# Down projection of an expert's last 32 slots on four quarters of the array's columns

## What is computed

```python
for e in range(N_EXPERTS):                                   # 16
    h = jax.nn.silu(xf @ w_gate[e]) * (xf @ w_up[e])         # 1024 -> 256
    out = out + gate[:, e:e + 1] * (h @ w_down[e])           # 256 -> 1024
x = layer_norm(ALPHA * x + out, ln2_g, ln2_b)
```

## Time and profile before

| | us |
|---|---|
| timed executions | 1508.08, 1513.96, 1527.37 |
| span of the profiled execution | 1520.2 |
| TensorE busy in the span | 1318.4 |
| first to last matmul of the experts | 1114.6 to 1439.3 |
| first gather of `combine` | 1446.2 |

### The profile page before, as it was taken

The page is one execution under the profiler, slowest core; times in us unless marked ns, Lnnn a source line. Parts: engine busy times, 40 slices in busy tenths (PEclk is TensorE's granted clock), DMA queues, the critical chain, the costliest instruction groups (busy, mean ns, idle before and its releaser), DMA issues. The chain is left out here.

```text
span 1520.2 us, 16147 instructions
## 1 busy us (share of the span) xinstructions
PE 1318.4 (87%) x5597; PEld 813.6 (54%) x5597; DVE 775.7 (51%) x1787; ACT 398.4 (26%) x805; POOL 431.7 (28%) x460
## 2 busy tenths in 40 slices
PE   5898899999999999999898997996289999999800
PEld 2566565755656656656654544653156666666500
DVE  0024125778778878988897988333300000000078
ACT  1142424324324224224314212311011111111111
POOL 5103024052151251261055012002231111113487
PEclk9999899999999898999898988575679999999955
DMA  8966645536543443443333333001078766667163
GB/s 272 313 200 210 231 145 179 173 108 201 155 159 123 146 147 112 146 147 108 113 113 122 110 94 118 1 14 29 4 252 301 235 218 234 211 203 250 35 221 121
DMA packets 146265, 238.60 MB, mean 157 GB/s; under 512 B 17211, under 2 KB 117474, under 8 KB 146194
## 3 DMA queue, kind: packets, MB, share of 16 engines
q1 hardware_dynamic: 131298, 197.66, 40.3%
q0 software_dynamic: 10064, 29.16, 5.9%
q10 hardware_dynamic: 4832, 10.88, 2.3%
HBM read 211.38 MB, written 26.29 MB: 156 GB/s over the span
## 5 line engine op out<-in xcount | busy, mean ns | idle before, releaser
L1188 PE MATMUL bank_pair<-win,xT 128*128 128x384 f32 (+7 forms) x1152 | 450.6, 542 | 14.8 <-DMA win<-in_w_in 13.7
L1188 PEld LDWEIGHTS bank_pair<-win,xT 128*128 128x128 f32 (+1 forms) x1152 | 213.3, 193 | 192.0 <-issue 100.9
L897 DVE MAX8 top<-score 128x8 f32<-128x384 f32 (+6 forms) x201 | 174.9, 870 | 4.0
L898 DVE MATCH_REPLACE8 score<-top,score 128x384 f32<-128x384 f32 (+6 forms) x201 | 171.9, 855 | 0.0
L1282 PE MATMUL bank_pair<-w_out,yT 128*128 128x512 f32 (+1 forms) x288 | 131.2, 610 | 0.4 <-ACT yT L623 0.4
L1641 DVE COPY rows<-bank_pair 32x1024 f32<-32x1024 f32 x16 | 19.4, 1212 | 170.3 <-PE bank_pair L1677 170.3
L567 POOL TENSOR_TENSOR small<-small,pexp 128x4 f32<-128x4 f32 (+1 forms) x9 | 9.4, 1049 | 335.9 <-DVE small L1078 335.9
L1677 PE MATMUL bank_pair<-wd,hT 128*128 128x512 f32 (+1 forms) x192 | 98.8, 653 | 0.0
L1551 POOL DMA_INDIRECT xg<-x_rows,ids x32 | 30.1, 941 | 229.1 <-PE bank_pair L1656 215.9
L1282 PEld LDWEIGHTS bank_pair<-w_out,yT 128*128 128x128 f32 (+1 forms) x288 | 52.8, 186 | 74.0 <-issue 72.2
L1142 PE MATMUL bank_pair<-ident,lm 128*128 128x128 f32 (+2 forms) x234 | 43.2, 312 | 45.8 <-ACT lm L733 15.8
(11 more groups left out here) (339 smaller groups left out, 2091.7 us busy)
## 6 DMA issues: line engine op xcount, KB each, us to landing
win<-in_w_in SPq DMA_DIRECT2D x90, 768.0 KB, 4.4
win<-in_w_in SPq DMA_DIRECT2D x18, 1024.0 KB, 5.3
win<-in_w_in SPq DMA_DIRECT2D x18, 840.0 KB, 5.2
win<-in_w_in SPq DMA_DIRECT2D x18, 800.0 KB, 4.6
wg<-in_w_exp_gate SPq DMA_DIRECT2D x12, 1024.0 KB, 6.2
wu<-in_w_exp_up SPq DMA_DIRECT2D x12, 1024.0 KB, 9.4
wd<-in_w_exp_down SPq DMA_DIRECT2D x12, 1024.0 KB, 11.1
expert_rows<-rows ACTq DMA_DIRECT2D x16, 512.0 KB, 3.3
```

Of the source, the lines that this page charges most:

```text
L897: step(V.max(top8[0:n], sc))
L898: step(V.match_replace(sc, top8[0:n], sc, NEG))
L1188: last = mmul(zb[0:n, 0:w], xT[:, kk, 0:n], win[:, i % NWIN, k, 0:w], start=(kk == 0), stop=(kk == KD - 1))
```

## The change

The 32 slots of OB are computed on all four quarters of the array's columns. Quarter `q` (columns 32q to 32q + 31) holds the same 32 columns of `hT` and multiplies the quarter `q` of `wd`'s 1024 columns (`DQ` = 256 of them), so that its output lies on partitions 32q to 32q + 31 of PSUM: 128 partitions of 256 instead of 32 partitions of 1024. There are 8 matmuls with 256 moving columns where there were 4 with 512, that is 16 MATMUL records instead of 8. OA is done with both halves `f` first, then OB with both. VectorE's copy takes 128 x 256, and the store writes each slot's row in four pieces of 1 KB instead of one of 4 KB.

```diff
+QB = 128 // CB
+DQ = D // QB
@@ ScalarE
-                    act.dma_start(rows_e[128:CAP, bass.ds(e, 1), :].rearrange("s one d -> s (one d)"), rows[j % 2][0:CB, 1, :]).then_inc(S(f"rows_stored{j % 2}"), 16)
+                    act.dma_start(rows_e[128:CAP, bass.ds(e, 1), :].rearrange("s one (q d) -> q s (one d)", q=QB),
+                                  rows[j % 2][:, 1, 0:DQ]).then_inc(S(f"rows_stored{j % 2}"), 16)
@@ VectorE
-                        V.tensor_copy(rows[j % 2][0:CB, 1, :], OB[0:CB, :]).then_inc(S("ob_copied"), 1)
+                        V.tensor_copy(rows[j % 2][:, 1, 0:DQ], OB[:, 0:DQ]).then_inc(S("ob_copied"), 1)
@@ TensorE
+                    pe.wait_ge(S("oa_copied"), e + 1)
                     for f in range(2):
                         pe.wait_ge(S("h_ready"), e * 2 + (f + 3))
-                        for out, c0, nb, sem in ((OA, 0, 128, "oa"), (OB, 128, CB, "ob")):
-                            if f == 0:
-                                pe.wait_ge(S(sem + "_copied"), e + 1)
-                            for c in range(2):
-                                last = E.matmul(out[0:nb, 512 * c:512 * c + 512], hT[:, f, c0:c0 + nb], wd[j][:, f, 512 * c:512 * c + 512],
-                                                start=(f == 0), stop=(f == 1))
-                            if f == 1:
-                                last.then_inc(S(sem + "_ps"), 1)
+                        for c in range(2):
+                            last = E.matmul(OA[:, 512 * c:512 * c + 512], hT[:, f, 0:128], wd[j][:, f, 512 * c:512 * c + 512],
+                                            start=(f == 0), stop=(f == 1))
+                    last.then_inc(S("oa_ps"), 1)
+
+                    pe.wait_ge(S("ob_copied"), e + 1)
+                    for f in range(2):
+                        for q in range(QB):
+                            last = E.matmul(OB[CB * q:CB * q + CB, 0:DQ], hT[:, f, 128:CAP], wd[j][:, f, DQ * q:DQ * q + DQ],
+                                            start=(f == 0), stop=(f == 1))
+                    last.then_inc(S("ob_ps"), 1)
```

## The result

The change takes 1465.89 us in the median of four executions (1457.91 to 1472.87), where the kernel before took 1513.89 beside it; the ratio is 0.9662, with a 95% interval from 0.9621 to 0.9704. A second measurement, beside one of the experiments, gave 0.967 [0.9618, 0.9723]. The profiled execution has a span of 1470.9 us where before had 1520.2, that is 49.3 less.

The account below looks back on a forecast made before the run. TensorE's work bounds the experts' stretch: 16 x (2.56 + 0.31) = 45.9, plus 0.8, plus 6.6, makes 53.3 us off 1513.96, so 1461 us. Likeliest case 1453 to 1474; up to 1485, about 8 in 10.

Parts of the forecast that it names:

- part 1: OB's streaming in the down projection: four quarters run at once, 0.88 us instead of 3.44, saving 2.56 us a body.
- part 2: Order in the down projection: OA, then OB, leaves two changes of shape instead of four, saving 0.31 us a body.
- two halves in L1397: Sign for part 1: L1397's heads alternate between array halves and overlap fully, a pair each 0.08 us; assumed for four quarters.
- The two rules of the Trainium skill: Against OB's overlap: weight loads overlap matmuls only across row groups (sum about nothing); matmuls start and end in program order (1480).
- strict order: Within rival two at a time: OB's records start strictly in order, 8 or 9 rounds, about 1480 us; rival's chance 0.17.
- part 5: Clock falls behind the experts' transposes: three instead of seven, 6.6 us saved; bounds 11.5 saved to 13.1 lost; softest term.
- part 3: OB's copy and store: copy 0.40 us instead of 1.21, saving 0.8 us once before `combine`; store's effect taken as 0.
- part 4: Shorter body of 16.84 us squeezes weight loads, gathers and GpSimd's scaling; all stay covered, cost 0, GpSimd's cover some 4 us.

Follow-up runs that it names:

- the run with the order alone: Against the kernel before: OA with both f, then OB with both f, OB still on one quarter; ratio 1.0054 [1.0017, 1.0092].
- the quarters outside: Against the change: OB's loops turned round, both f for each quarter before the next quarter; ratio 0.9732 [0.9678, 0.9786].
- four stores: Against the change: OB's store issued as four stores, one for each quarter, instead of one with outer dimension four; 1474.0 us in one execution.

## Why the prediction was right

The forecast was 53.3 us less (1461 us); the medians differ by 48.0 (1465.89 us), the profiled executions by 49.3, and the ratio makes 51.

- The streaming (part 1): right to 0.01 us. Together with the order (part 2) a body was to shrink by 2.87 us to 16.84; it did. The order's share is the 0.31 us of the run with the order alone, the quarters' share the rest. What the prediction drew from two halves in L1397 holds for four quarters. The two rules of the Trainium skill that it weighed (TensorE: Matmul & The Clock Gate, Part 3, "What overlaps and what doesn't") don't hold here: four records with four weight loads on the same rows start together, and four rounds are measured where strict order would need nine, or thirteen with the quarters outside.
- The clock (part 5): three falls taken, three measured, and that is luck. From the start of the first to the start of the last matmul of the experts it is 324.2 us before (1114.6 to 1438.9; the table's 1439.3 is neither that start nor the end, 1439.5) and 272.1 after (1116.2 to 1388.3), 52.1 less, for 45.9 + 6.6 = 52.5. But the three was chosen between none and 15 without a working, and the argument for fewer falls, that a body of another length doesn't keep step with them, isn't borne out: the run with the order alone, a body shorter by 0.31 us, got three falls more, and bodies of 16.84 us with seven or ten would have cost 6.6 or 11.5 us more. That the falls need the transposes in one piece is shown by cutting them; how many falls a length of body meets is not explained by the runs (19.71 us: seven; 19.39 and 19.41: ten; 17.68: six; 16.86 and 16.84: three).
- The end (part 3): the term that was mis-sized. It was to save 0.8 us and cost 1.9 (9.14 us from the last matmul's start to the gather for 7.27). The copy is right (0.42 us for 0.40); the store was set at nothing, within 1 us, and cost 1.9 + 0.8 = 2.7. The step that failed is that it looked at the size of the pieces and not at the shape of the store, whose outer dimension of four keeps it to four DMA engines.
- What the shorter body squeezes (part 4): nothing became late. GpSimd's scaling ends at 1385.04, 3.7 us before VectorE's last copy starts, for some 4 expected, and the DMA engines' share of 0.76 over the stretch (0.65 before) left TensorE waiting no more than before:

```profile
1360.36 24.68 POOL L1564 TENSOR_SCALAR xr<-xr 128x1024 f32<-128x1024 f32 x9 [19.31 <-DMA b<-in_ln_b]
```

The time that a gather has was worked out wrongly, though harmlessly: it is asked for when the transposes of expert `e - 1` are done and needed for those of `e + 1`, two bodies less the transposes themselves, 30 us, not 11.

- The rest of the difference is 1.6 us by which the trunk, which isn't touched, ended later in the profiled execution of the change, less 0.6 us in `combine`: 52.1 - 1.9 - 1.6 + 0.6 = 49.2. The trunk moves by much more between executions. The first matmul of the experts starts at these times in the run with the order alone and in that with four stores:

```profile
L1668 PE MATMUL bank_pair<-xgT,win x256: 299/299/630, 1101.1 to 1357.3; 128*128 128x160 f32 x128
```

```profile
L1670 PE MATMUL bank_pair<-xgT,win x256: 299/299/629, 1118.7 to 1334.1; 128*128 128x160 f32 x128
```

That is 17.6 us apart for the same trunk, nearly as much as the 19 us between the kernel before's own executions. Up to these starts TensorE has 4078 matmul records in both, busy for 982.95 us at a mean granted clock of 0.89 in the first and for 998.52 us at 0.88 in the second: most of the difference is TensorE's time, and the granted clock is the lower one there; why it differs isn't shown. A term of 5 us is read from the stretch and not from the total.

## What to carry to other kernels

Where TensorE is the bound and an output fills only a quarter of the array's columns, spread its moving columns over the four quarters: the matmuls run at once, in either order of the loops. Look at the granted clock of every body before believing a saving: one kernel here lost three falls' worth for the 0.31 us that each body gained, and cutting the long run of transposes in two won 15.8 us by the trace, where the order's 5.0 had been lost again. And when a store's access pattern is rearranged, count the entries of its outer dimension; in these runs they set how many DMA engines it ran on, up to 16.

## What the runs showed of the hardware that was not expected

- A store whose outer dimension has four entries is spread over four of the 16 DMA engines, by its completions, and 128 KB of it held up the end by 1.5 us against four stores over all of them (9.14 us in three traces, 7.67 in one).
- Records for another quarter of the columns pass by three records that wait for theirs (1.02 us for 16 records with four in a row on each quarter, 1.00 in rounds).
- A kernel with less work on TensorE can take as long as before: 19.39 us a body at full clock for 19.71, ten falls for seven, 324.3 us for 324.2.
